# Value projections of 512 columns, layer 0's keys first, scores that wait per bank, bias table and modulation slabs in threes

## The reference

```
h = x * (1 + scale) + shift          # scale, shift, gate: silu(c) @ mod_w[i] (1024 x 6144), for latents and context
x = LayerNorm(alpha * x + gate * (mixer(h) @ w_o))
h = x * (1 + scale2) + shift2
x = LayerNorm(alpha * x + gate2 * ((silu(u_gate) * u_val) @ w_down)),  u = conv3(h @ w_up)   # 1024 -> 5632, 2816 -> 1024
```

## Time and profile before

| | us |
|---|---|
| median of 3 runs | 2580.01 |
| lowest, highest | 2573.11, 2580.82 |
| the profiled execution | 2578.89 |
| its span, first to last instruction | 2577.1 |
| PE busy | 2438.4 |
| DVE busy | 1392.1 |
| ACT busy | 1134.2 |

### The profile page before, as it was taken

One profiled execution on the slowest core, in us unless ns is written; L12 is line 12 of the kernel. 1 busy time (PEld: TensorE's weight loads), 2 busy tenths in 40 slices (PEclk: granted clock), 3 DMA queues, 4 the chain that ended last, 5 costly groups with the idle time before them and its releaser, 6 DMA issues.

```text
span 2577.1 us, 37987 instructions
## 1 busy us (share of the span) xinstructions
PE 2438.4 (95%) x15310; PEld 1960.5 (76%) x15310; DVE 1392.1 (54%) x2099; ACT 1134.2 (44%) x1936; POOL 334.9 (13%) x270
## 2 busy tenths in 40 slices
PE   6999899999999898999999999899999999978997
PEld 3655877778789558777788878787777888947997
DVE  2375665453444776555534336766555435477874
ACT  3375543333342565333323444454333325276663
POOL 0000311110100003111101003331111111002111
PEclk8999899999999999999999999999999999999998
DMA  7712366663232002665632421025666335603663
GB/s 246 213 42 81 92 182 186 180 178 105 78 99 88 28 25 66 187 181 180 176 104 80 112 69 43 2 67 150 186 185 181 113 92 105 149 17 101 186 180 99
DMA packets 500995, 311.39 MB, mean 121 GB/s; under 512 B 24194, under 2 KB 499762, under 8 KB 500692
## 3 DMA queue, kind: packets, MB, share of 16 engines
q1 hardware_dynamic: 498048, 307.39, 41.0%
q10 hardware_dynamic: 2772, 1.56, 0.2%
HBM read 307.87 MB, written 1.05 MB: 120 GB/s over the span
## 4 chain that ended last, share of the span: by engine, by line
PE 82%; DVE 7%; ACT 5%; DMA 3%; issue 2%; SPq 1%; ACTq 0%; DVEq 0%
PE bank L1543 69%; PE bank L1595 4%; PE bank L1722 2%; PE bank L1770 1%; DMA slab_raw<-in_d_w_qkv 1%; PE bank L1742 1%; DMA slab_raw<-in_a_w_o 1%; ACT slab_hi L526 1%; DVE stat L1184 1%; DVE slab_lo L960 1%; ACT p L707 1%; ACT hb L541 1%; DVE q_part L1243 1%; DMA slab_raw<-in_mod_w 1%; ACT pt L719 1%
## 5 line engine op out<-in xcount | busy, mean ns | idle before, releaser
L1543 PE MATMUL bank<-h_hi,slab_hi 128*128 128x512 f32 (+1 forms) x2416 | 859.6, 356 | 38.7 <-DVE slab_lo L960 26.5
L1543 PE MATMUL bank<-h_lo,slab_hi 128*128 128x512 f32 (+1 forms) x2416 | 836.9, 346 | 0.0
L960 DVE TENSOR_TENSOR slab_lo<-slab_raw,slab_hi 128x1024 fp32r<-128x1024 f32 (+1 forms) x388 | 538.6, 1390 | 552.1 <-ACT slab_hi L526 550.7
L1543 PE MATMUL bank<-h_hi,slab_lo 128*128 128x512 f32 (+1 forms) x2416 | 836.6, 346 | 0.0
L526 ACT ACTIVATE slab_hi<-slab_raw 128x1024 fp32r<-128x1024 f32 (+1 forms) x388 | 401.5, 1036 | 529.1 <-PE bank L1543 264.1
L1543 PEld LDWEIGHTS bank<-h_hi,slab_hi 128*128 128x128 f32 x2416 | 465.1, 193 | 150.0 <-issue 90.2
L1543 PEld LDWEIGHTS bank<-h_hi,slab_lo 128*128 128x128 f32 x2416 | 465.3, 193 | 55.9
L1543 PEld LDWEIGHTS bank<-h_lo,slab_hi 128*128 128x128 f32 x2416 | 465.9, 193 | 50.0 <-issue 0.5
L929 ACT ACTIVATE conv<-bank,prm 128x512 f32<-128x512 f32 (+1 forms) x176 | 127.3, 723 | 355.1 <-PE bank L1543 354.8
L1543 PE MATMUL bank<-g_hi,slab_hi 128*128 128x512 f32 (+1 forms) x770 | 269.3, 350 | 2.1 <-ACT res_t L577 2.1
L1543 PE MATMUL bank<-g_hi,slab_lo 128*128 128x512 f32 (+1 forms) x770 | 267.2, 347 | 0.0
(11 more groups left out here) (218 smaller groups left out, 2744.0 us busy)
## 6 DMA issues: line engine op xcount, KB each, us to landing
slab_raw<-in_mod_w SPq DMA_DIRECT2D x192, 512.0 KB, 4.5
slab_raw<-in_ffn_w_up SPq DMA_DIRECT2D x176, 512.0 KB, 4.6
slab_raw<-in_ffn_w_down SPq DMA_DIRECT2D x64, 512.0 KB, 4.1
slab_raw<-in_ffn_w_down SPq DMA_DIRECT2D x32, 384.0 KB, 3.5
slab_raw<-in_b_w_qkv SPq DMA_DIRECT2D x24, 512.0 KB, 3.8
slab_raw<-in_c_w_in SPq DMA_DIRECT2D x24, 512.0 KB, 3.8
slab_raw<-in_d_w_qkv SPq DMA_DIRECT2D x24, 512.0 KB, 7.0
slab_raw<-in_a_w_qkv SPq DMA_DIRECT2D x12, 512.0 KB, 5.4
```

The costliest lines, as they stand in the source:

```text
L960: nc.vector.tensor_tensor(wlo[slot][:, 0:w], raw[of][:, 0:w], whi[slot][:, 0:w].bitcast(f32), ALU.subtract).then_inc(s_lo, 1)
L1543: ins = mm(out, l, r, start=first and n == 0, stop=last and n == 2)
```

## The change

1. In layers 1 to 3 the values are made in two groups of 512 channels. A slab then holds two row tiles of 512 columns (`vw`), and for each slab all four token tiles are advanced, in four banks at once, by 2 x 3 matmuls of 512 columns (`v_wide`). A new semaphore `v_full` counts token tiles that are ready, and DVE copies a bank of 512 columns each time (`wide_values`, after the second and the fourth step of its loop).
2. Layer 0 projects its two key tiles first (`qkv_tiles(0)`), and ACT copies the keys to `kd` behind the roots of tiles 5 to 8, two copies for each tile.
3. Scores wait for what each uses: the first four for the value copy out of their own bank (`values_copied`), those of layer 0 for their own query tile, and the first product with the values for all copies. The wait for the window additions moves from PE to DVE, and these additions move to steps 0, 1 and 2 (two of them) of the loop.
4. The bias table is issued in threes: three blocks ahead of each of layer 3's slabs 6 to 9, and the window ahead of slab 10.
5. Modulation slabs: three at a time behind 16 of the 40 up tiles (tiles 4, 6, 9, 11, 14 and so on); in layer 0's projection four at a time behind tiles 1, 3, 5, 7 and 9, in place of four behind tile 1 and two behind each of tiles 2 to 9.

```diff
 def mods_after(phase, tile):
     if phase == "qkv":
-        return (range(0), range(0, 4))[tile] if tile < 2 else range(2 * tile, 2 * tile + 2)
+        return range(0) if tile % 2 == 0 else range(2 * tile - 2, 2 * tile + 2)
...
-    return [m for m in range(48) if 4 + m * (2 * FT - 4) // 48 == 2 * j + k] if i + 1 < layers else []
+    return [m for m in range(48) if 4 + m // 3 * (2 * FT - 4) // 16 == 2 * j + k] if i + 1 < layers else []
 def qkv_tiles(i):
+    if i == 0:
+        return [8, 9] + list(range(8))
...
-                    add(("v", name, 2048 + 256 * g, q))
+                    add(("vw", name, 2048 + NB * (g // 2), 2 * (g % 2) + q))
...
+            if kind == "vw":
+                _, name, c, q = s
+                return a[name][0, 2 * q * P:(2 * q + 2) * P, c:c + NB].rearrange("(k p) c -> p k c", p=P), 2
...
-                if 0 <= table <= 12:
-                    if table == 0:
-                        sp.wait_ge(s_hlo, h_steps(6, 1, PAIRS - 1) + 1)
+                if table == 0:
+                    sp.wait_ge(s_hlo, h_steps(6, 1, PAIRS - 1) + 1)
+                for table in range(3 * table, min(3 * table + 3, 13)) if 0 <= table < 5 else ():
...
+                    if 5 <= ft < 9:
+                        kt, j = divmod(ft - 5, 2)
+                        act.wait_ge(S["qk_ready"], kt + 1)
+                        for half in range(2):
+                            ins = nc.scalar.activation(kd[HD * half:HD * half + HD, 2 * kt + j, :],
+                                                       qk[HD * j:HD * j + HD, 8 + kt, :], ACT.Copy)
+                        ins.then_inc(s_kd, 1)
                 roots(9)
...
-                act.wait_ge(S["qk_ready"], 10)
-                for kt in range(2):
-                    for j in range(2):
...
...
+            def v_out(i, n, fg):
+                for g in range(4):
                     splits_to(n + 2 * g + 1 + AHEAD)
-                    values(n, fg, g)
-                    if masked_bias:
+                    if g % 2:
+                        wide_values(i, n, fg, g // 2)
+                    for g in ((0,), (1,), (2, 3), ())[g] if i == 3 else ():
                         dve.wait_ge(s_bias_in, 16 * 13)
...
+            def wide_values(i, n, fg, g):
+                for tt in range(4):
+                    if tt < 3:
+                        dve.wait_ge(att[i]["v_full"], 3 * g + tt + 1)
+                    else:
+                        dve.wait_ge(s_used, n + 4 * g + 4)
+                    nc.vector.tensor_copy(v_tok[:, tt, NB * g:NB * g + NB], bank[(fg + 4 * g + tt) % 4][:]
                                           ).then_inc(s_free["dve"], 1)
...
                 if i == 3:
+                    dve.wait_ge(s_window, 4)
                     add_bias(0)
...
+            def v_wide(i, n, fg, between={}):
+                for g in range(2):
+                    for q in range(4):
+                        slab = n + 4 * g + q
+                        split_ready(slab)
+                        for tt in range(4):
+                            place = 16 * g + 4 * q + tt
+                            if place % 2 == 0 and place // 2 in between:
+                                between[place // 2]()
+                            if q == 0:
+                                group_free(fg + 4 * g + tt)
+                            for k in range(2):
+                                wc, tc = slice(NB * k, NB * k + NB), slice(tt * P, tt * P + P)
+                                ins = three(bank[(fg + 4 * g + tt) % 4][:], whi[slab % SLOTS][:, wc], wlo[slab % SLOTS][:, wc],
+                                            h_hi[:, 2 * q + k, tc], h_lo[:, 2 * q + k, tc], q == k == 0, q == 3 and k == 1,
+                                            moving_w=True)
+                            if tt == 3:
                                 ins.then_inc(s_used, 1)
-                    n, fg = n + 2, fg + 2
+                            elif q == 3:
+                                ins.then_inc(att[i]["v_full"], 1)
...
-                    n_last = freed[start["wo", i][1] - 9]
-                    pe.wait_ge(s_free["act"], n_last[1])
-                    pe.wait_ge(s_window, 4)
+                    pe.wait_ge(s_free["act"], freed[start["wo", i][1] - 9][1])
+                elif i == 1:
+                    pe.wait_ge(S["qk_ready"], 16)
                 else:
-                    pe.wait_ge(S["qk_ready"], 10 if i == 0 else 16)
-                if i == 0:
-                    pe.wait_ge(s_kd, 1)
-                pe.wait_ge(s_free["dve"], freed[start["wo", i][1] - 1][1])
+                    pe.wait_ge(s_kd, 4)
+                def values_copied(b):
+                    last = start["wo", i][1] - 1
+                    pe.wait_ge(s_free["dve"], freed[last - (last - b) % 4][1])
...
+                        if i == 0 and hd % 2 == 0 and s == 0:
+                            pe.wait_ge(S["qk_ready"], 3 + qt)
+                        if maps * u + m < 4:
+                            values_copied(maps * u + m)
...
+                    if w == 0:
+                        pe.wait_ge(s_free["dve"], freed[start["wo", i][1] - 1][1])
```

More of the change, by code:

```diff
@@ L394, in width @@
         def width(s):
-            return {"v": SLAB, "up": SLAB}.get(s[0]) or s[4] * P
+            return {"v": SLAB, "vw": SLAB, "up": SLAB}.get(s[0]) or s[4] * P
         def mirrored(ap):
@@ L1139, in qkv_norm_rope @@
                 rope(S, 9, bank[5][:, 0:LAT], rope_t)
-                v_out(n, fg + 10, 1)
+                splits_to(n + 1 + AHEAD)
+                values(n, fg + 10)
                 mod_evacuate(0, 4, 9, 1)
@@ L1284, in qkv_gla @@
                     split(n + 16 + 2 * g + 1 + AHEAD)
-                    values(n + 16, fg + 16, g)
+                    if g % 2:
+                        wide_values(2, n + 16, fg + 16, g // 2)
             def gla(n_v):
@@ L1619, in stats, with v_project @@
                 mm(LN_SQ[:, c], average, sq[e % 2][:, c], start=False, stop=True).then_inc(s_stats, 1)
-            def v_project(n, fg, groups, between={}):
-                for g in range(groups):
-                    split_ready(n + 1)
-                    for tt in range(4):
-                        if 4 * g + tt in between:
-                            between[4 * g + tt]()
-                        if tt % 2 == 0:
-                            group_free(fg + tt // 2)
-                        out = bank[(fg + tt // 2) % 4][:, 256 * (tt % 2):256 * (tt % 2) + 256]
-                        for k in range(DT):
-                            slot, wc = (n + k // 4) % SLOTS, slice(256 * (k % 4), 256 * (k % 4) + 256)
-                            tc = slice(tt * P, tt * P + P)
-                            ins = three(out, whi[slot][:, wc], wlo[slot][:, wc], h_hi[:, k, tc], h_lo[:, k, tc],
-                                        k == 0, k == DT - 1, moving_w=True)
-                            if tt == 3 and k % 4 == 3:
+            def v_project(n, fg, between):
+                split_ready(n + 1)
+                for tt in range(4):
+                    if tt in between:
+                        between[tt]()
+                    if tt % 2 == 0:
+                        group_free(fg + tt // 2)
+                    out = bank[(fg + tt // 2) % 4][:, 256 * (tt % 2):256 * (tt % 2) + 256]
+                    for k in range(DT):
+                        slot, wc = (n + k // 4) % SLOTS, slice(256 * (k % 4), 256 * (k % 4) + 256)
+                        tc = slice(tt * P, tt * P + P)
+                        ins = three(out, whi[slot][:, wc], wlo[slot][:, wc], h_hi[:, k, tc], h_lo[:, k, tc],
+                                    k == 0, k == DT - 1, moving_w=True)
+                        if tt == 3 and k % 4 == 3:
+                            ins.then_inc(s_used, 1)
@@ L1635, in v_project @@
                                 ins.then_inc(s_used, 1)
-                    n, fg = n + 2, fg + 2
+                            elif q == 3:
+                                ins.then_inc(att[i]["v_full"], 1)
             def swapped(S, ft, ps):
-                mm(ps, swap, qk[:, ft, CTX:T], start=True, stop=True).then_inc(S["swapped"], 1)
+                mm(ps, swap, qk[:, qkv_tiles(0 if S is att[0] else 1)[ft], CTX:T], start=True, stop=True).then_inc(S["swapped"], 1)
             def qkv_norm_rope(n, fg):
@@ L1673, in qkv_norm_rope @@
                 squares(9)
[L1674 removed]
+                v_project(n, fg + 10, between={1: lambda: turn(8), 3: lambda: turn(9)})
                 mod_turn(1)
@@ L1684, in qkv_plain @@
                         turn(S, ft - 4, fg)
-                v_project(n + 16, fg + 16, 4,
-                          between={x: functools.partial(turn, S, 12 + x, fg) for x in range(4)} if i == 1 else {})
+                v_wide(i, n + 16, fg + 16,
+                       between={x: functools.partial(turn, S, 12 + x, fg) for x in range(4)} if i == 1 else {})
             def turn(S, ft, fg):
```

38 lines of the change are left out of this document (17 added, 21 removed).

## The result

The changed kernel takes **2543.8 us** (median; 2542.7 to 2547.1) beside 2580.4 for the kernel before in the same session: a ratio of 0.986, 95% interval 0.9844 to 0.9877, so 36.6 us less.

The account below looks back on a forecast made before the run. PE, busy 2438.4 of 2577.1 us, was taken as the bound, with its idle waits. Terms -7.9 + 1.4 - 18.0 + 8.8 - 5.7 - 2.2 - 4.5 + 11.5 = -16.6 us gave 2563 us, range 2551 to 2574.

Parts of the forecast that it names:

- Modulation slabs in threes: Up stages of three layers: 16 gaps with three slabs cost PE less than 32 with one and 8 with two; -18.0 us.
- 0.68 in all: Up stages: PE's price of one modulation slab with its gap, 0.43 us for the slab and 0.25 for the gap.
- Bias table: Layer 3's queries: bursts at 2.5 us a block delay slabs, idles of 3.8 and 6.4 us; +11.5 us (0 to 16).
- Rival A: Layer 3: the table's burst delays nothing, as blocks share the DMA engines with slabs; 2552 us, chance 0.10.
- B: Layer 0 doesn't stop, as the load behind the first of four slabs arrives well before tile end; 2555 us, chance 0.07.
- E: Up stages: threes make PE wait for modulation slabs, 48 groups at 0.96 us, +46 us; 2609 us, chance 0.06.
- Rival D: Layers 3 and 0 both reach their upper bounds (16 and 12 us); 2571 us, or 2572 with layer 2's copies; chance 0.10.
- Layer 0's projection: Modulation slabs in fours: fewer gaps, but late rotations and a 5.6 us stop ahead of squares(9); +8.8 us (-1.0 to +12).
- Values, matmuls: Layers 1 to 3: 576 matmuls of 512 columns at 0.2267 us replace 1152 of 256 at 0.1202; -7.9 us.
- rival C: Layers 1 to 3: wide value matmuls save no fixed part and cost what two narrow ones do; 2571 us, chance 0.04.
- Waits: Idle ahead of first scores goes: layer 0 with keys first -5.7 us, layer 1 -2.2, layer 3 -4.5.
- Layer 2: Wide values there bring 1.2 us of idle and 0.2 for last copies, +1.4 us; the layer -1.2 us in all.

Follow-up runs that it names:

- twos: Up-projection modulation slabs in twos behind 24 of the 40 tiles, on the kernel before: 2561.6 us beside 2579.1, ratio 0.993.
- threes: Only the up-projection modulation slabs in threes behind 16 tiles, on the kernel before: 2551.0 us beside 2578.1, ratio 0.9891.
- fours: Kernel after with layer 0's dense split moved last and up-projection modulation slabs in fours behind 12 tiles: 2531.1 us, ratio 0.9813.
- sixes: Kernel after with six bias table blocks ahead of each of slabs 6 and 7, window ahead of slab 8: 2551.5 us, ratio 0.9892.

## Why the prediction was wrong, step by step

- **Modulation slabs in threes: right mechanism, term mis-sized** (-18.0 forecast, -28.5 measured; about 1.3 of that is layer 1's part alone, where the clock came back sooner: a granted clock of 0.67 and then 1.00 in the 9 us from some 10 us into the part on, for 0.50 and 0.76 before; 72 x 0.37 is 26.6). The step that failed is "0.68 in all", and with it 0.25 for a gap. It counted 0.57 to the next matmul and 0.11 behind that. It left out the near side of the gap: a tile between two groups takes 5.67 us from its first matmul to the slabs, where 24 x 0.2267 is 5.44. So a gap is (0.57 - 0.43) + (5.67 - 5.44) = 0.14 + 0.23 = 0.37. Most of the 0.23 is seen in these rows of the kernel after (PE's timeline, one gap with threes): 0.34 from the first projection matmul to the second, and 0.32 from the last one to the slabs, where 0.23 is usual; that is 0.20 of it, and the last 0.03 lies in rows not looked at one by one.

```profile
347.35 0.39 PE L1562 MATMUL bank<-h_hi,slab_lo 128*128 128x512 f32 x1
347.67 1.50 PE L1614 MATMUL bank<-slab_raw,cond_wide 128*32 128x256 f32 x24
349.10 0.50 PE L1562 MATMUL bank<-h_hi,slab_hi 128*128 128x512 f32 x1
349.44 0.39 PE L1562 MATMUL bank<-h_lo,slab_hi 128*128 128x512 f32 x1
```

  The distance from one group to the same group a period later would have shown it; twos, threes and fours bear it out.
- **Bias table: step failed** (+11.5 forecast; +2.5 to +3 by the traces that differ in it alone). The order of the queue was right, and ACT waits as forecast. The step that failed is "so a block is 2.5": a pair's 4.27 less 1.77 for the slab, as if a slab behind a block cost no more than one at full rate. By the landings it was the other way round, some 1.8 for the block and 2.5 for the slab. The bursts move the blocks alone: with 1.7 for each of eight more, the forecast's own sum puts slab 9's high half 54.5 us into the stage and not 60.9. It began at 51.4, and PE's reserve covers most of what is left, so that one idle of 1.85 us stands where two of 3.8 and 6.4 were forecast. The bounds on record (0.9 to 2.8) hold 1.7. And a second step was missing: the values' first group wants one slab fewer, worth 2 to 3 us in layer 3. What sets the slab's 2.0 to 2.5 us behind a block stays open.
- **Rival A** (the burst delays nothing) comes near the right size in its own term, yet the burst does delay: slabs are 5.0 to 8.6 us apart, behind three blocks each, and sixes cost 8 to 10 us. A little of its reason is in the landings, for the first block issued behind slab 7 landed at 2149.35 and slab 7 at 2150.08. Rivals B and E are out: layer 0 stops, and no up group waits. Rival D is out as well, since layer 3's term was not near its upper bound.
- **Layer 0's projection: right** (+7.9, and 1.4 at the lower clock behind it, for +8.8). The stop was 5.72 (5.6 forecast), rotations 0.64 to 0.81 (0.9).
- **Values, matmuls: right**: 0.2269 us. This goes against the formula that the prediction quoted from the Trainium skill (TensorE: Matmul & The Clock Gate, Back-to-back issue gap), which gives 0.2158 for an isolated gap; the rows decide, and rival C is out.
- **Waits: right** in layers 1 and 3. In layer 1 the values took 44.97 us for 47.41, and from the last of them to the first score are 0.32 us for 2.61: -2.4 and -2.3, where -2.6 and -2.2 were forecast. In layer 0 no wait is left ahead of the scores either, but the -6.2 beside the forecast's -5.7 is in part luck of this pair: over all traces it is -3.9, near the lower bound on record (-3.7).
- **Layer 2: off, and mostly not by the change** (+1.1 for -1.2). Its values took 54.99 us for 55.94, and the start of the row that ends the stop is 0.44 later behind them: -0.5 in all, for which every kernel with wide values has the same within 0.1 us. The remaining +1.6 lies between that stop and the layer's output projection, 97.75 us for 96.15. There the code is the same in all kernels, and the traces take 96.1 to 99.8 us, so this part is not shown to be the change's.

## What to carry to other kernels

Price a switch between two kinds of matmul by a whole period (from one group to the next of its kind, less the bare work), not by the rows next to it, for both sides of the gap pay; then gather the small group into fewer gaps until a buffer ring objects. Where a gathered group empties a ring of buffers, look for what stands behind the next load in an in-order engine: here the split went behind the work that PE wanted, and a stop that had cost 9 us was gone with the fours kept. A distance between two rows that wait for different loads prices the pair of loads and not one of them; read when each load landed before a term of 11 us rests on the split. And where a stage differs by 2 or 3 us between kernels that have the same code there, compare it over several of them.

## What was not expected of the hardware

- A gap between projection matmuls and modulation slabs (unsplit float32, 32 columns stationary) costs 0.37 us of PE that no row shows as idle: PE stands at 140.00 of 140.00 busy, and some 22 such gaps in that stretch take 8 us.
- Loads of 256 KB in runs of 64 floats landed 1.7 us apart in bursts of six, and 1.6 to 1.8 us (medians) behind a slab of 512 KB when the two took turns. The slab behind such a block took 2.0 to 2.5 us, where the three slabs behind the table in the kernel before landed 1.48, 1.37 and 1.33 us behind the slab ahead of them. Pairs of block and slab were 4.27 us apart in the kernel before, 3.66 in the run with keys first alone, and 3.34 with wide values alone, all with the same loads at that place. What sets it there stays open.
- After a stop the granted clock stays low for a stretch that differs from run to run. Layer 3's stop of 7.66 us ahead of the last feed-forward part is in both kernels, and what follows it took 1.1 us more in the kernel after. Over all fourteen traces this last stage takes one of two lengths, 212.2 to 212.4 us in seven and 213.3 to 213.5 in seven, whatever the change. So the +1.1 in the table is not the change's. In rows of the kernel after, and then of before, from the first matmul on:

```profile
2327.40:2331.40 4.00, 3.94 (x18) 3.97 (x19) 2.50 (x4) 3.90 (x8) 0.00 (x0) 0.50 0.00 0
2331.40:2335.40 4.00, 4.00 (x28) 4.00 (x27) 1.92 (x2) 2.49 (x3) 0.00 (x0) 0.72 0.00 0
```
```profile
2364.80:2368.80 4.00, 3.98 (x22) 4.00 (x23) 2.46 (x4) 3.90 (x8) 0.00 (x0) 0.61 0.02 4
```
- From layer 0's first scores to its feed-forward part the runs took 143.9 to 148.6 us, with the same work in most of them. A small part are modulation loads that PE waits for; the rest was not settled, and it is why the traces' stages, and not only the medians, were compared.
